# Routing from the raw residual stream during the output projection, and expert weights released by quarters, in a two-layer transformer step

## The reference, cut to what matters

```
x  = x + g1 * (merged @ w_out)
h2 = rmsnorm(x, norm2) * (1 + sc2) + sh2          # sc2, sh2 from c @ w_ada, per channel and group
scores = sigmoid(h2 @ router_w)                   # 16 experts in 4 groups of 4
biased = scores + router_bias
group_score = sum of the 2 best of each group; best_group = argmax
top_idx = 2 best experts inside best_group; gates = their scores / their sum
y  = sum_e gates_e * ((silu(h2 @ w_gate[e]) * (h2 @ w_up[e])) @ w_down[e])
x  = x + g2 * y
```

## Time and profile before

| | us |
|---|---|
| median of 3 runs (lowest, highest) | 1094.32 (1094.08, 1097.36) |
| the profiled execution | 1093.94 |
| its span in the trace | 1092.1 |
| PE busy | 998.8 (91%) |
| DVE, ACT, POOL busy | 350.4, 235.3, 85.0 |
| DMA, queue of SP | 311.21 MB, 70.1% of 16 engines' span |

### The profile page before, as it was taken

The page is one execution under the profiler, slowest core; times in us unless marked ns, Lnnn a source line. Parts: engine busy times, 40 slices in busy tenths (PEclk is TensorE's granted clock), DMA queues, the critical chain, the costliest instruction groups (busy, mean ns, idle before and its releaser), DMA issues.

```text
span 1092.1 us, 13619 instructions
## 1 busy us (share of the span) xinstructions
PE 998.8 (91%) x5130; PEld 596.5 (55%) x5130; DVE 350.4 (32%) x930; ACT 235.3 (22%) x514; POOL 85.0 (8%) x52
## 2 busy tenths in 40 slices
PE   5899999989959998999899999999896999899987
PEld 2348876657835533443354588777684564344333
DVE  2125113772171022222251421248425302222224
ACT  2103222420121211111131222342103121111111
POOL 0000004720000000000000000066000000000000
PEclk9899999999989999999999999999998899999999
DMA  9965244079686799999999533230579379999992
GB/s 393 427 267 199 82 154 154 1 303 387 266 329 279 303 422 422 371 422 422 422 427 385 207 112 148 78 154 26 216 322 365 137 322 409 422 370 422 421 421 120
DMA packets 36483, 314.27 MB, mean 288 GB/s; under 512 B 4112, under 2 KB 4240, under 8 KB 5072
## 3 DMA queue, kind: packets, MB, share of 16 engines
q1 hardware_dynamic: 35856, 311.21, 70.1%
q0 software_dynamic: 576, 2.36, 0.5%
HBM read 311.72 MB, written 1.84 MB: 287 GB/s over the span
## 4 chain that ended last, share of the span: by engine, by line
PE 71%; DMA 13%; DVE 9%; ACT 4%; issue 2%; SPq 1%; ACTq 0%; DVEq 0%
PE ps L868 17%; DMA ring<-w_gu 11%; PE ps L475 10%; PE ps L559 8%; PE ps L880 6%; PE ps L739 5%; PE ps L825 3%; PE ps L728 3%; PE ps L841 3%; PE ps L577 3%; DMA ring<-w_ada 2%; PE ps L670 2%; PE ps L455 2%; PE ps L488 1%; PE ps L608 1%
## 5 line engine op out<-in xcount | busy, mean ns | idle before, releaser
L868 PE MATMUL ps<-ring,tmq 128*64 128x512 f32 x928 | 212.4, 598 | 19.6 <-DMA ring<-w_gu 17.9
L868 PEld LDWEIGHTS ps<-ring,tmq 128*64 128x64 f32 x928 | 67.7, 138 | 145.1 <-issue 123.1
L475 PE MATMUL ps<-more,ring 128*128 128x256 f32 x512 | 114.3, 381 | 0.5 <-ACT more L937 0.5
L880 PE MATMUL ps<-ring,tmq 128*64 128x512 f32 x512 | 113.4, 595 | 0.0
L937 ACT ACTIVATE tmq<-ps 128x256 f32<-128x256 f32 (+3 forms) x124 | 56.0, 465 | 226.7 <-PE ps L880 91.2
L475 PEld LDWEIGHTS ps<-more,ring 128*128 128x128 f32 x512 | 96.1, 190 | 15.5 <-issue 2.5
L559 PE MATMUL ps<-ring,more 128*128 128x512 f32 (+1 forms) x256 | 99.1, 548 | 1.6 <-DVE more L1280 1.6
L1604 DVE TENSOR_TENSOR tmq<-tmq,ps 128x256 f32<-128x256 f32 x32 | 13.5, 422 | 221.5 <-ACT tmq L1176 221.5
L559 PEld LDWEIGHTS ps<-ring,more 128*128 128x128 f32 x256 | 48.8, 192 | 50.7 <-issue 48.9
L880 PEld LDWEIGHTS ps<-ring,tmq 128*64 128x64 f32 x512 | 35.3, 137 | 66.6 <-issue 66.3
L1615 DVE SCALAR_TENSOR_TENSOR x<-ps,mod,x 128x128 f32<-128x128 f32 x256 | 67.6, 342 | 1.9 <-PE ps L825 1.9
(11 more groups left out here) (220 smaller groups left out, 1023.0 us busy)
## 6 DMA issues: line engine op xcount, KB each, us to landing
ring<-w_gu SPq DMA_DIRECT2D x116, 1024.0 KB, 13.4
ring<-w_down SPq DMA_DIRECT2D x64, 1024.0 KB, 12.9
ring<-w_ada SPq DMA_DIRECT2D x24, 2048.0 KB, 10.3
ring<-w_in SPq DMA_DIRECT2D x16, 2048.0 KB, 19.6
ring<-w_out SPq DMA_DIRECT2D x4, 2048.0 KB, 10.5
more<-w_gu SPq DMA_DIRECT2D x8, 1024.0 KB, 9.2
cst<-consts SPq DMA_DIRECT2D x2, 2048.0 KB, 28.2
ring<-w_pa SPq DMA_DIRECT2D x2, 2048.0 KB, 8.3
```

The source lines that it names most:

```text
L475: mm = pe.matmul(ps[:, 5, i * NT:(i + 1) * NT], w[:, k, m * P:(m + 1) * P], h[:, k, :], start=k == 0, stop=k == KT - 1)
L868: mm = pe.matmul(ps[r:r + SLOTS, half, :].rearrange("p (j n) -> p j n", j=2), hg[:, k, r:r + SLOTS], gu_unit(l, kh, e, in_more)[:, :, kk, ...
L880: mm = pe.matmul(ps[r:r + SLOTS, 2 + n, :], at_[:, k, r:r + SLOTS], down_unit(l, k // 2)[:, e, k % 2, n * 512:(n + 1) * 512], start=k == 0 ...
```

## The change

1. **Router on raw x.** The weights of the router are multiplied by the norm's gain in advance (`wra`, POOL), so the logits are taken from `x` itself, one matmul per tile inside the output projection (`route`). Since the inverse root is one number per token, it is applied to the 16 logits of a token after the turn; the shift's part comes from `shift_w` and a sum by ones.
2. **Token-major second norm.** DVE makes `xa` = x times gain per tile, PE turns it inside the output projection (`turn_x`), the shift is spread over the tokens by a matmul of ones with a diagonal matrix (`diag`, POOL; `shift_rows`), ACT copies that to `h2tok`, and DVE adds the turned tile times the inverse root (`token_rows_of`). The full-size norm, its modulation, the turn of h2 and its four copies go. Sums of squares: POOL adds the squared tiles 0 to 6, PE makes two columns (`token_sums`).
3. **Choice of experts.** `first_max` goes; each expert is compared with the others of its group (`beat`), wins are counted, and `sel` is signalled ahead of `before_e`, which is now a scan. The counting matmuls fall from 7 plus 2 to 4 plus 2.
4. **ada units.** The window's first is computed ahead of the pb projection, the second between pb and the output projection; in layer 0 the other two follow `token_sums`, with their biases ahead of the one-hots of all rows.
5. **Quarters.** Gate/up weights are laid out, multiplied and released in quarters of the contraction, `m_rows` counting three times a pair; SP issues 1 MB parts of two units in turn.

```diff
-        out += [(l, "pb", 0), (l, "out", 0), (l, "out", 1)]
-        out += [(ll, "ada", a) for ll, a in window(l)]
+        win = [(ll, "ada", a) for ll, a in window(l)]
+        out += [win[0], (l, "pb", 0), win[1], (l, "out", 0), (l, "out", 1)] + win[2:]
...
+                for units in ((0, 1), (2, 3), (4,), (5,)):
+                    for part in range(2):
+                        for u in units:
+                            if u >= first:
+                                sp.wait_ge(*waits[u][part])
+                                expert_part(l, pr, u, part, moe_full[l][u])
...
-                return [(m_rows[l], q + 1)] * 2 + [(m_gu[l][1], q + 1)] * 2 + [(m_dn[l][0], q + 1), (m_dn[l][1], q + 1)]
+                rows = [(m_rows[l], q * 3 + i) for i in (-1, 0, 1)]
+                return ([rows[:2]] * 2 + [[rows[2], (m_gu[l][1], q + 1)]] * 2 +
+                        [[(m_dn[l][half], q + 1)] * 2 for half in range(2)])
...
+            def token_sums(l):
+                pe.wait_ge(rw_ready, RW * (l + 1))
+                for s in range(S):
+                    c = slice(s * T, (s + 1) * T)
+                    pe.matmul(ps[:, 0, s:s + 1], h[:, 0, c], ones[:, 0:1], start=True, stop=False)
...
+                    mm = pe.matmul(ps[:, 0, s:s + 1], h[:, KT - 1, c], ones[:, 0:1], start=False, stop=True)
+                mm.then_inc(ssum, 1)
+            def route(l, k):
+                pe.wait_ge(x_mid, MID * l + k + 1)
+                r = 2 * 32 * (k % 2)
+                mm = pe.matmul(ps[r:r + 64, 1, 0:NT], wra[:, k, :, :].rearrange("p s n -> p (s n)"), x[:, k, :], start=k < 2,
+                               stop=k >= KT - 2)
+            def turn_x(l, k):
+                pe.wait_ge(x_mid, MID * l + k + 2)
+                for s in range(S):
+                    mm = pe.transpose(ps[:, 2 + 2 * (k // 4) + s, (k % 4) * P:(k % 4 + 1) * P],
+                                      xa[:, k % XA_SLOTS, s * T:(s + 1) * T], ident)
+            def shift_rows(l, j):
...
+                pe.matmul(ps[:, 0, :], ones, diag[:, j % 2, :, :].rearrange("p a n -> p (a n)"), start=True, stop=True)
...
                 for b in range(KT):
                     w = full(l, "out", b // 4)
+                    if b % 2 == 0:
+                        shift_rows(l, b // 2)
...
                     mm.then_inc(out_mm, 1)
+                    if b >= 1:
+                        route(l, b - 1)
                     if b >= 2:
-                        norm_sum_mid(l, b - 2)
-                norm_sum_mid(l, KT - 2)
-                norm_sum_mid(l, KT - 1)
-                win = window(l)
-                ada_a(*win[0])
-                ada_b(*win[0])
-                ada_a(*win[1])
+                        turn_x(l, b - 2)
+                pe.wait_ge(sq_act, SQUARES * l + 4 + 6)
                 for k in range(KT):
+                    pe.matmul(ps[:, 0, 32:64], ones, shift_w[:, k, :, :].rearrange("p s e -> p (s e)"),
+                              start=k == 0, stop=k == KT - 1)
+                turn_x(l, 6)
+                route(l, 7)
+                token_sums(l)
+                turn_x(l, 7)
...
-                        for half in range(2):
-                            for kk in range(KH):
+                        for part in range(2):
+                            for half in range(2):
+                                for kk in range(KH // 2):
...
+                token_rows_of(0, 0)
...
+                dve.tensor_tensor_scan(before_e[:, 1:NE], sel[:, 0, 0:NE - 1], sel[:, 1, 0:NE - 1], 0.0, ALU.add,
+                                       ALU.add).then_inc(sel_ready, 1)
+                for w in window(l)[2:3]:
+                    ada_bias(*w)
+                for half, s in ((0, 1), (1, 0), (1, 1)):
+                    token_rows_of(half, s)
...
                 ins.then_inc(m_rowhot[l], 1)
+                for w in window(l)[3:]:
+                    ada_bias(*w)
...
-                for w in window(l)[2:]:
-                    ada_bias(*w)
```

More of the change, by code:

```diff
@@ L55 @@
 SQUARES = 3 + KT
+XA_SLOTS = 4
+MID = KT + 1
+RW = 5 + KT - 2
 TMW = LR0
@@ L151 @@
 PLACE = {key: n for n, key in enumerate(ORDER)}
-BEFORE = [PLACE[(w[0], "ada", w[1])] + 1 for w in (window(l)[-1] for l in range(LAYERS))]
+BEFORE = [max(PLACE[(l, "out", 1)], *(PLACE[(ll, "ada", a)] for ll, a in window(l))) + 1 for l in range(LAYERS)]
 def build(nc, xT, consts, params, lparams, w_ada, w_in, w_pa, w_pb, w_out, w_gu, w_down,
@@ L410, in _ @@
                         sp.dma_start(cst[:, C_LATE:CW], consts[:, C_LATE:CW]).then_inc(in_d, 16)
[L412 to L416, removed]
+                for u in range(RING):
+                    sp.wait_ge(*used(n - RING + u))
+                    for part in range(2):
+                        expert_part(l, 0, u, part, moe_full[l][u])
+                    if u == 1:
+                        sp.wait_ge(merged, 4 * (l + 1))
+                        more_unit(l, 0)
+                        more_unit(l, 2)
+                sp.wait_ge(ssum, 2 * l + 2)
                 more_unit(l, 1)
@@ L722, in _ @@
                 flush()
+                win = window(l)
+                ada_a(*win[0])
                 w = full(l, "pb", 0)
@@ L769, in _ @@
-                ada_b(*win[1])
-                for w in win[2:3]:
-                    ada_a(*w)
-                pe.wait_ge(sel_ready, l + 1)
-                sel = rt[:, 0, :, :]
-                for s in range(S):
-                    pe.matmul(ps[:, 1, 64 + s * NE:64 + (s + 1) * NE], C("before"), sel[:, s, :], start=True, stop=False)
-                    if s:
-                        pe.matmul(ps[:, 1, 64 + NE:64 + 2 * NE], ones, sel[:, 0, :], start=False, stop=False)
-                    mm = pe.matmul(ps[:, 1, 64 + s * NE:64 + (s + 1) * NE], ones, before_e, start=False, stop=True)
+                        turn_x(l, b - 2)
@@ new lines, in _ @@
+                mm.then_inc(r_log, 1)
+                if win[2:]:
+                    ada_a(*win[2])
+                    ada_b(*win[2])
+                    ada_a(*win[3])
+                pe.wait_ge(sel_ready, 2 * l + 1)
+                sel = rt[:, 0, :, :]
+                pe.matmul(ps[:, 1, 64:64 + 2 * NE], C("before"), rs[:, 0:2 * NE], start=True, stop=False)
+                pe.matmul(ps[:, 1, 64 + NE:64 + 2 * NE], ones, sel[:, 0, :], start=False, stop=False)
+                pe.wait_ge(sel_ready, 2 * l + 2)
@@ new lines, in _, with token_rows_of @@
+                for s in range(S):
+                    ins = dve.scalar_tensor_tensor(rt[:, 1, s, :], rt[:, 1, s, :], v[:, s:s + 1],
+                                                   ps[:, 0, 32 + s * NE:32 + (s + 1) * NE], ALU.mult, ALU.add)
+                ins.then_inc(r_sum, 1)
+                def token_rows_of(half, s):
+                    if half == 0:
+                        dve.wait_ge(h2_t, KT * l + 4)
+                    else:
+                        dve.wait_ge(h2_t, KT * (l + 1))
+                    row = h2tok[:, s, half * 512:(half + 1) * 512]
+                    dve.scalar_tensor_tensor(row, ps[:, 2 + 2 * half + s, :], v[:, s:s + 1], row, ALU.mult,
+                                             ALU.add).then_inc(h2_ready, 1)
```

278 lines of the change are left out of this document (159 added, 119 removed).

## The result

| | before | after |
|---|---|---|
| median of 4 runs each (lowest to highest) | 1094.2 (1092.43 to 1097.36) | 1086.58 (1085.87 to 1087.01) |
| span of the profiled execution | 1092.1 | 1085.2 |
| PE, POOL busy in the span | 998.8, 85.0 | 1009.1, 105.8 |

The ratio of the times is 0.9923, 95% interval 0.9899 to 0.9947: 7.6 us (0.8%) faster. Forecast were 14.4 us, 1080.0 with the range 1072 to 1088. So the direction and the stated range hold, and about half of the gain is missing: the time lies outside the 1076 to 1084 that the favoured case A gave itself, in the part of the range that was there for B's dearer gather and links and for narrow matmuls at 0.43.

What follows compares the result with a forecast made beforehand. Expert stages were held by PE first, then weight loads, after gaps where norm, router and choice run serially. Layer 0 -10.85, layer 1 -1.75 and quarters -1.8 gave -14.4 us: from 1093.94 to 1079.5, as median 1080, range 1072 to 1088.

Steps and rivals of the forecast that it cites:

- case A: Favoured case, chance 0.62: all terms as summed, 1080 us, own range 1076 to 1084.
- B's dearer gather and links: Rival, chance 0.14: layer 0's gather also at half clock, a chain link or two 1 us dearer: 1084.7.
- The chain behind the projection: From t0, the projection's last block end: choice at 9.8 us, experts at t0 + 18.5 (layer 0), + 20.8 (layer 1).
- Rival D: Chance 0.05: shift and token sums cost only by their columns, 2.1 us less a layer, 1076.
- Rivals E and F: E (0.06): loads end when they did, 1094. F (0.05): output half's product doesn't fit under 1.75 us, 1096 to 1097.
- The ada units ahead of t0: Before the output projection's end, PE gets two ada units and their turns, 4.05 us in each layer.
- The projection: Output projection: shifts 3.4, six route matmuls 2.6, turns 1.05, less norm sums 2.15: 4.9 us longer.
- the 10 us that the prediction had set as a sign of being wrong: End of the output projection (t0): a move beyond 10 us, from POOL or DVE being late, would refute the prediction.
- The gather of layer 0: Ahead of layer 0's experts: 3.5 us at full clock, as PE is no longer idle than 2 us.
- The quarters: Expert gate/up loads: releasing by quarters gives 0.9 us a layer (0 to 3.5), 1.8 in all.
- the first dry spell: DMA queue at 380 to 384, 313 GB/s: quarters cover it; the second, 444 to 452, waits for down and stays.
- Earlier experts, earlier end: Expert stages: starting X earlier ends X earlier, stalls included; pair 0's down units free 33.9 us after the start.

Runs made afterwards that it cites:

- e4: Kernel after with both ada units of layer 1 moved back behind the output projection: 1083.16 us (ratio 0.9887).
- e5: Kernel after with the router products' weights 128 columns wide (upper 64 zeros), all adding into one tile: 1080.56 us (ratio 0.9851).
- e6: Kernel after with the 64-wide router products and the turns put in two groups, behind block 5 and the last block: 1077.63 us (ratio 0.9827).
- e10: Kernel after with e6's groups, e4's late ada units and four filler matmuls ahead of each gather: 1071.75 us (ratio 0.9782).
- e9: Kernel after with e6's groups and e4's late ada units, without fillers: 1074.39 us (ratio 0.9815).
- e11: e9 with gate/up laid out, multiplied and released by halves instead of quarters: 1073.59 us (ratio 0.9804).

## Why the prediction was right, and half of it was not

- **The chain behind the projection** (right). The choice came 10.2 us after t0 (forecast 9.8), the gather of layer 0 at t0 + 14.2 (14.1), 0.15 us behind the last one-hot, with no bias in between, and the experts of layer 1 at t0 + 20.7 (20.8). The last is in part luck: the gather there started 0.5 late (t0 + 14.2, forecast 13.7) and was 0.5 shorter (5.78, forecast 6.3). The narrow sums cost what L776 had said: L808's sixteen records take 1.70 us start to start, 0.21 a matmul of 32 columns. Rival D, narrow matmuls by their columns (the Trainium skill, TensorE: Matmul & The Clock Gate, section "What happens when you issue a matmul"), is refuted here. Rivals E and F did not come about: the stages' ends moved with their starts, and of the first turns of the pairs none waits for the product (pair 0's, at 341.70, has no idle ahead of it; only the second turn of pair 0 waits, 1.03 us in each layer).
- **The ada units ahead of t0** (right): +3.9 against 4.05. e4 shows that in layer 1 they need not stand there.
- **The projection, a term mis-sized.** "six `route` matmuls before t0, 0.43 each" and turns at 0.21 a pair, with the blocks unchanged at 3.5, gave 4.9; measured 6.9 in each layer. A product alone between two blocks costs 0.58, the turns behind it 0.27, and the block 3.55. e5 takes 0.3 us per product, 1.9 per layer, back by the shape of the weights alone, which is nearly the whole term; e6 takes 2.2 back, 1.5 of it by fewer changes and 0.7 by products that run in pairs. The price per record had been taken from a stretch in which all weights are 128 wide, and the rows in which a narrower load follows a full-width one (L455 at 298.88) were left aside. In both layers this is 4.0 of the missing 7.5 us. By this term t0 also moved past the 10 us that the prediction had set as a sign of being wrong.
- **The gather of layer 0, the rival B in part.** Taken at full clock (3.5), measured 5.34, at half clock for most of it: 1.8 us. The reason given, "no longer idle than 2 us", held to the letter and was no protection: PE idled 1.98 us. B's dearer links did not come: the choice was 0.4 late and the last one-hot on time.
- **The quarters** (mechanism right, size not resolved). As forecast the first dry spell is gone (426 GB/s from 372.6 to 376.6) and the second is left; it grew: 249 GB/s instead of 292, and 270 in e1, the kernel after without quarters. The likely reading is that loads that start sooner wait the longer for the same down units; no run shows it. Three pairs of profiles give 1.1, 1.2 and 1.5 us less waiting in both layers together, against 1.8; three pairs of times give gains of 1.7 and 1.6 us and a loss of 0.8. By layer the waits of gate/up fell by 1.2 us in layer 0 and 0.1 in layer 1, against 0.9 each. In layer 0 of the kernel after the half-clock stretch in pair 7 (8.78 for 7.09) covers all of it.
- **Earlier experts, earlier end** (right). Down of pair 0 was free 33.8 us after the experts' start (33.9), and the stages' ends moved with their starts.

So of the 17.9 us that came off layer 0's gap 10.8 were paid ahead of it, and in layer 1 the two cancel; the whole gain is layer 0's, where the bias of the ada units no longer stands between choice and gather (there the gather started 9.0 us behind the last one-hot). The fastest kernel of the experiments, e10, is 22.7 us below the kernel before (1071.75 against 1094.4): what the grouping of e6, the cover of e4 and the fillers brought on top, some 15 us, is more than the change itself brought. Weights of one width (e5) are not in e10; the two together were not tried.

## What to carry to other kernels

A small product that is put between full-width matmuls must be priced with the loads around it: give it weights as wide as its neighbours', or put several behind one another, which for 64-wide weights also lets two run at once. Work moved off a serial chain pays only what it costs at its new place; ask for every piece whether there is cover behind the chain (the ada units of layer 1, the turns of tiles 4 to 7) before paying for it ahead. When two kernels differ by 1 to 2 us in a thousand, compare waits in their profiles, and subtract the stretches that ran at half clock in only one of them.

## What the runs showed of the hardware

- A matmul with 64-column weights behind one with 128 starts its load only when it starts itself: 0.33 us of idle ahead of the load and 0.39 ahead of the next 128-wide one. With 128-wide weights both are gone.
- In a group, products that go to the two halves of the array's columns in turn run at 0.29 us each (five in e6), where a 128-wide product of the same 256 columns takes 0.43. Two of them run at once: their records start 0.007 us apart, and the pairs mostly 0.22 us apart. The fifth has no partner, and the change into and out of the group adds some 0.15.
- A float32 matmul of 32 columns costs 0.21 us, nearly as much as one of 128 (the gather at full clock: 16 matmuls of 128 columns in 3.74 to 3.81 us, 0.23 to 0.24 each).
- The place of the half-clock stretch is not fixed by the program: one kernel, e10, took 1067.86 to 1077.67 us with a mean granted clock between 0.984 and 0.994, and the same 0.91 us of idle ahead of layer 1's gather was followed by full clock in e9 and by half clock in e11. What decides where it falls stays open.
- POOL's 512-column product took 1.04 us and its 256-column addition 0.73 inside the projection. The addition lies within the bounds set from the 896-column row (0.6 to 2.1), the product below its 1.2, and PE never waited for them.
